# Where the second block's modulation is computed: VectorE row products in three feed-forward loops, an early half of the first norm, and turned rows

## The reference, cut to what matters

```python
cond = jax.nn.silu(c)
for i in range(DEPTH_2):                                  # 4
    mod = cond @ ada_w[i] + ada_b[i]                      # 1024 x 6144 weights, 24 MB
    sh_a, sc_a, g_a, sh_f, sc_f, g_f = jnp.split(mod, 6, axis=-1)
    h = modulate_2(rms_norm_2(x, norm_g[i, 0]), sh_a, sc_a)
    ...                                                   # y = mla, stick-breaking, retention, mla for i = 0..3
    x = x + g_a[:, None, :] * rms_norm_2(y, norm_g[i, 1])
    h = modulate_2(rms_norm_2(x, norm_g[i, 2]), sh_f, sc_f)
    y = jnp.square(jax.nn.relu(h @ ffn_w1[i])) @ ffn_w2[i]
    x = x + g_f[:, None, :] * rms_norm_2(y, norm_g[i, 3])
```

## Time and profile before

| | us |
|---|---|
| runs | 3032.50, 3034.65 and 3042.34, median 3034.65 |
| the profiled execution's own time | 3033.94 |
| its span, first to last instruction | 3031.9 |
| start of the span to the first matmul of `ab_in` | 35.1 |
| block 0: turn of its norm to the end of its attention, output projection and second norm | 1565.8 to 1720 |
| block 0: feed-forward | 1720 to 1900 |
| block 1: mixer, then feed-forward | 1904 to 2100, then to 2277 |
| block 2: mixer, then feed-forward | 2280 to 2505, then to 2720 |
| block 3: mixer, then feed-forward | 2724 to 2848, then to 3026 |

### The profile page before, as it was taken

How to read it: one execution, slowest core, us unless ns; L and a number is a source line. 1 busy time by engine, 2 the same in 40 slices (tenths; PEclk the granted TensorE clock), 3 DMA queues, 4 the chain that set the end, 5 groups by cost and what they waited for, 6 DMA issues and landing times.

```text
span 3031.9 us, 34611 instructions
## 1 busy us (share of the span) xinstructions
PE 2731.1 (90%) x13420; PEld 1704.6 (56%) x13420; DVE 1193.3 (39%) x2164; ACT 925.6 (31%) x1648; POOL 39.4 (1%) x51
## 2 busy tenths in 40 slices
PE   7999887877899889878789899998999999999999
PEld 3433422222564442222254688857888988875787
DVE  1762300001242320000033667547677465444776
ACT  2112211110212320000023544545445444444543
POOL 0010000000000000000000000000000000000000
PEclk9999999999999989999999999999999999999999
DMA  8673499999822859999986254681546425663152
GB/s 366 257 311 154 185 428 428 428 428 429 356 89 95 322 226 428 428 428 429 428 345 275 124 194 162 264 331 52 194 179 262 153 111 203 279 254 131 56 194 97
DMA packets 59496, 796.20 MB, mean 263 GB/s; under 512 B 8636, under 2 KB 9916, under 8 KB 10748
## 3 DMA queue, kind: packets, MB, share of 16 engines
q1 hardware_dynamic: 55664, 790.13, 63.4%
q10 hardware_dynamic: 3724, 4.59, 0.4%
HBM read 793.64 MB, written 1.05 MB: 262 GB/s over the span
## 4 chain that ended last, share of the span: by engine, by line
PE 74%; DMA 18%; DVE 4%; ACT 3%; issue 1%; SPq 0%; ACTq 0%; DVEq 0%; POOL 0%; POOLq 0%
PE banks L1982 12%; DMA ring<-in_t_up 7%; DMA ring<-in_t_down 7%; PE banks L1482 7%; PE banks L1999 6%; PE banks L913 6%; PE banks L1498 5%; PE banks L798 5%; PE banks L928 4%; PE banks L1357 4%; PE banks L2002 3%; PE banks L767 3%; PE banks L2006 3%; DMA arena<-in_t_gate 2%; PE banks L787 1%
## 5 line engine op out<-in xcount | busy, mean ns | idle before, releaser
L1482 PE MATMUL banks<-ring,arena 128*64 128x512 f32 x1920 | 477.2, 621 | 95.9 <-DMA ring<-in_t_up 52.2
L3043 DVE TENSOR_TENSOR ring_lo<-ring,w_hi 128x1024 fp32r<-128x1024 f32 x256 | 312.4, 1224 | 227.8 <-ACT w_hi L2414 226.7
L2414 ACT CAST w_hi<-ring 128x1024 fp32r<-128x1024 f32 x256 | 268.2, 1054 | 383.5 <-PE banks L1982 188.1
L1482 PEld LDWEIGHTS banks<-ring,arena 128*64 128x64 f32 x1920 | 161.7, 143 | 386.2 <-issue 346.6
L2601 DVE TENSOR_TENSOR arena<-arena,banks 128x512 f32<-128x512 f32 x32 | 22.0, 687 | 794.9 <-PE banks L1482 794.9
L1999 PE MATMUL banks<-u_pair,w_hi 128*128 128x512 f32 x768 | 273.3, 400 | 3.6 <-DVE ring_lo L3043 3.1
L2119 ACT COPY arena<-banks 32x512 f32 x96 | 55.3, 576 | 607.3 <-PE banks L1498 606.6
L1498 PE MATMUL banks<-ring,arena 128*64 128x512 f32 x896 | 210.3, 624 | 28.4 <-DMA ring<-in_t_down 17.1
L2002 PE MATMUL banks<-u_pair,ring_lo 128*128 128x256 f32 x768 | 215.4, 281 | 0.0
L1982 PE MATMUL banks<-w_hi,ffn_h_hi 128*128 128x512 f32 x512 | 202.3, 395 | 0.0
L1982 PE MATMUL banks<-ring_lo,ffn_h_hi 128*128 128x512 f32 x512 | 199.5, 390 | 0.0
(11 more groups left out here) (362 smaller groups left out, 4073.5 us busy)
## 6 DMA issues: line engine op xcount, KB each, us to landing
ring<-in_t_ada SPq DMA_DIRECT2D x72, 2048.0 KB, 10.0
ring<-in_t_ffn SPq DMA_DIRECT2D x64, 2048.0 KB, 8.5
ring<-in_t_gate SPq DMA_DIRECT2D x60, 2048.0 KB, 22.0
ring<-in_t_up SPq DMA_DIRECT2D x60, 2048.0 KB, 22.1
ring<-in_t_down SPq DMA_DIRECT2D x56, 2048.0 KB, 21.6
ring<-in_t_ret_in SPq DMA_DIRECT2D x12, 2048.0 KB, 8.5
arena<-in_t_down SPq DMA_DIRECT2D x8, 2048.0 KB, 31.2
ring<-in_t_in_cd SPq DMA_DIRECT2D x6, 2048.0 KB, 16.1
```

What stands on the lines that cost most here:

```text
L1482: mm = nc.tensor.matmul(PS[64 * h:64 * h + 64, f.bank, :], x_cur[:, b, k, :], wview(un[h0 + h], KC)[:, k, :], start=(k == 0), stop=(k == K ...
L2414: nc.scalar.copy(w_hi[:, n % 4], w).then_inc(S("ffn_w_hi"), 1)
L3043: TT(w_lo, w, w_hi[:, n % 4].bitcast(F32), ALU.subtract).then_inc(S("ffn_w_lo"), 1)
```

## The change

1. `ada_w_2` of layers 1 to 3 is laid out transposed (`by_outputs`, `t_ada_dots`): a tile holds, for each of 128 outputs on the partitions, four rows of 1024 weights. Bytes and number of tiles stay the same.
2. Blocks 0, 1 and 2 (`DOTS`) each load the next block's twelve tiles in their feed-forward loop, three a pass, in three slots of their own (before, two). DVE multiplies each row of 1024 with `cond_row` and sums it (`dot_dve`): twelve of these a pass, after the steps of `DOT_STEPS` and one at the end, then a copy of twelve sums to `MOD`. The tiles in `mla_pe`, `stick_pe` and the feed-forward's PE pieces go, with their ACT copies and DVE sums.
3. `cond_row` is the conditioning vector along the free axis, the same on all partitions: eight PE transposes of a broadcast column before the second norm's turn (`cond_row_pe`) and two 512-column ACT copies, once in each of blocks 0 to 2.
4. The three loops are unpaired: `PAIRED` is `(3,)`. ACT rectifies, then squares twice (rounded to `ffn_h_hi` and in float32); DVE does only the subtraction.
5. Layer 0's first four tiles are split: tiles 0 and 2 (shift and scale of chunks 0 to 3) are loaded and computed first, then the first weight tile of `ab_in`, then tiles 1 and 3, whose PE work is put after chunks 1 and 2 of the first tile of `ab_in`. DVE and ACT do the gains of chunks 4 to 7 between their own chunks 3 and 4.
6. `gp_pe` uses transposes, not matmuls.

```diff
-        plan_ada("l0a", 0, 0, 4, [0, 1, 2, 3])
+        FRONT = (("l0a", (0, 2), [0, 1, 2, 3]), ("l0d", (1, 3), [4, 5, 6, 7]))
+        plan_ada(FRONT[0][0], 0, FRONT[0][1], FRONT[0][2])
...
                 ab_units += load(turn(1), units_of(a["t_in_ab"], j))
+                if n == 0:
+                    plan_ada(FRONT[1][0], 0, FRONT[1][1], FRONT[1][2])
...
-        ADA_IN_FFN = (2,)
-        PAIRED = (0, 1, 3)
+        DOTS = (0, 1, 2)
+        PAIRED = (3,)
...
             if more:
-                fa = lambda q: (SLOT, lambda it, v=a["t_ada"][i + 3], q=q: v[it * 3 + q])
+                fa = lambda q: (SLOT, lambda it, v=a["t_ada_dots"][i], q=q: v[it * 3 + q])
                 items = [f1(0), fa(0), f1(1), fa(1), f2(0), fa(2), f2(1)]
-                slots = [s[0], s[4], s[2], s[5], s[1], s[4], s[3]]
+                slots = [s[0], s[4], s[2], s[5], s[1], s[6], s[3]]
...
+                for q, u in enumerate(au):
+                    u.used = Mark(S("dot"), 48 * i + 4 * (q + 1), 12)
...
+        cond_row = region(W + 2048, [D])
+        dots = small[:, 12:24]
...
+        def cond_row_pe(pe, i):
+
+            for half, f in enumerate(plan[f"b{i}_cb"]):
+                f.open(pe)
+                for q in range(4):
+                    mm = nc.tensor.transpose(PS[:, f.bank, q * P:(q + 1) * P],
+                                             cond[:, 4 * half + q, 2:3].to_broadcast([P, P]), ident)
+                mm.then_inc(f.full.sem, 1)
...
-                    mm = nc.tensor.matmul(PS[:, f.bank, q * P:(q + 1) * P],
-                                          GP[:, i, which, k:k + 1].to_broadcast([P, P]), ident, start=True, stop=True)
+                    mm = nc.tensor.transpose(PS[:, f.bank, q * P:(q + 1) * P],
+                                             GP[:, i, which, k:k + 1].to_broadcast([P, P]), ident)
...
+                def late_tiles(q):
+
+                    if q == 1:
+                        ada_rows_pe(late[0], late_rows[0])
+                        ada_rows_pe(late[1], late_rows[1])
+                        ada_cols_pe(late_rows[0], late_cols[0], 0)
+                    if q == 2:
+                        ada_cols_pe(late_rows[1], late_cols[1], 1)
...
-                    if s % 2 == 1 and s < 16:
-                        tile_rows(4 + s // 2)
-                    if s % 2 == 0 and s < 17:
-                        tile_cols(3 + s // 2)
...
-                    if 2 <= s < 14:
-                        ada_rows_pe(plan[p + "ada_units"][s - 2], plan[p + "ada_rows"][s - 2])
-                    if 3 <= s < 15:
-                        ada_cols_pe(plan[p + "ada_rows"][s - 3], plan[p + "ada_cols"][s - 3], (s - 3) % 2, store=st_rows)
...
+                        if i in PAIRED:
+                            act.wait_ge(S("ffn_squared"), 32 * i + k + 1 + it * 8)
+                            nc.scalar.copy(h_hi, h).then_inc(S("ffn_h_hi"), 1)
+                        else:
+                            plan[p + "up"][k].free.wait(act, it)
+                            nc.scalar.activation(h_hi, h, ACT.Square).then_inc(S("ffn_h_hi"), 1)
+                            nc.scalar.activation(h, h, ACT.Square).then_inc(S("ffn_squared"), 1)
...
+                if i in DOTS:
+                    for half, f in enumerate(plan[p + "cb"]):
+                        copy_act(act, f, cond_row[:, half * 512:half * 512 + 512], PS[:, f.bank, :])
                 ffn_hi(i, 0, 0)
...
+            DOT_STEPS = (1, 2, 3, 4, 6, 8, 10, 12, 13, 14, 15)
+
+            def dot_dve(i, n, it):
+
+                u = plan[f"b{i}_dot_units"][n // 4]
+                if n % 4 == 0:
+                    u.landed.wait(dve, it)
+                w = ring[:, u.slot, (n % 4) * D:(n % 4 + 1) * D]
+                STT(w, w, 1.0, cond_row, ALU.mult, ALU.mult, accum_out=dots[:, n:n + 1]).then_inc(S("dot"), 1)
...
+                    if i in DOTS and n in DOT_STEPS:
+                        dot_dve(i, DOT_STEPS.index(n), it)
...
+                if i in DOTS:
+                    dot_dve(i, 11, it)
+                    dve.wait_ge(S("dot"), 48 * i + 12 + it * 12)
+                    V_.tensor_copy(MOD[:, bass.ds(192 + (i + 1) * 48 + it * 12, 12)], dots).then_inc(S("dot_kept"), 1)
+                    dve.wait_ge(S("dot_kept"), 4 * i + 1 + it)
```

More of the change, by code:

```diff
@@ L553, in block_program @@
                 plan[p + "units"] = us
-                fills(p + "scores", ([0, 1, 6] * 6)[:16] if i == 0 else [0, 1, 6, 7] * 4)
+                fills(p + "scores", [0, 1, 6, 7] * 4)
                 fills(p + "turn", [2, 3] * 8)
[L556 to L563, removed]
+                fills(p + "pv", [4, 5] * 4)
                 use_split(p + "out", load(turn(2), units_of(a["t_mla_out"][j], 0, 1)), "tokens", [0, 1, 2, 3],
@@ L569, in block_program @@
                 use_split(p + "v", load(turn(2), units_of(w, 4, 5)), "tokens", [4, 5, 6, 7], st_in_slots, p + "qk")
[L570 to L575, removed]
                 fills(p + "z", [0, 1] * 8)
@@ L592, in block_program @@
             fills(p + "fnorm", [4, 5, 6, 7])
-            more = i in ADA_IN_FFN
+            more = i in DOTS
+            if more:
+                fills(p + "cb", [0, 1])
             c0 = cursor[0]
@@ L712, in pieces, with scale_dve @@
             return [(k, s) for k in range(KC) for s in range(ns)]
-        def scale_dve(dve, c, layer, which, ns, x_first=False):
-            for k, s in pieces(ns, x_first):
+        def scale_dve(dve, c, layer, which, ns, x_first=False, late=None):
+            for n, (k, s) in enumerate(pieces(ns, x_first)):
+                if late is not None and n == 4 * ns:
+                    late()
                 t = slice(s * N, (s + 1) * N)
@@ L719, in scale_dve, with shift_act @@
                                                ALU.mult, ALU.mult).then_inc(S("u_scaled"), 1)
-        def shift_act(act, c, layer, which, ns, x_first=False):
-            for k, s in pieces(ns, x_first):
+        def shift_act(act, c, layer, which, ns, x_first=False, late=None):
+            for n, (k, s) in enumerate(pieces(ns, x_first)):
+                if late is not None and n == 4 * ns:
+                    late()
                 t = slice(s * N, (s + 1) * N)
@@ L2514, in ada_dve, with front_half @@
                     f.free.wait(dve)
-            ada_dve("l0a", 0, 0)
-            gains_first(0, 0, 4, (0,))
+            def front_half(half):
+                name, tiles, _ = FRONT[half]
+                fc = plan[f"ada_{name}_cols"]
+                for f, j in zip(fc, tiles):
+                    cols_dve(f, 8 * j, 0, 0, 2)
+                for f in fc:
+                    f.free.wait(dve)
+                at = 4 * half
+                m = MOD[:, 0:32].rearrange("p (w i s) -> p w i s", w=2, s=2)[:, :, at:at + 4, :]
+                b = cols("b_ada", 0, 16).rearrange("p (w i) -> p w i", w=2)[:, :, at:at + 4]
+                ch.do(TT(m, m, b.unsqueeze(3).to_broadcast([P, 2, 4, 2]), ALU.add))
+                ch.do(STT(AM[:, 2 * at:2 * at + 8].rearrange("p (k s) -> p k s", s=2), m[:, 1], 1.0,
+                          cols("g_mix", at, 4).unsqueeze(2).to_broadcast([P, 4, 2]), ALU.add, ALU.mult))
+            front_half(0)
             def trig(x, k, rows, quarter):
@@ L3099, in _ @@
                 split_u_dve(dve, c, p + "fnorm", "ffn")
+                if i in DOTS:
+                    plan[p + "cb"][-1].free.wait(dve)
                 with dve.Fori(0, 3) as it:
```

119 lines of the change are left out of this document (33 added, 86 removed).

## The result

The changed kernel takes 3002.67 us (median of four runs, 3000.16 to 3003.30), the kernel before beside it 3033.57: a ratio of 0.9891, with a 95% interval of 0.9871 to 0.9911. This is 31 us faster, less than half of the 71 us forecast, and 7.7 us above the range's upper end. The profiled execution took 3000.16 us, its span is 2998.1 us, and its mean granted clock 0.954, against 0.972 before.

What follows compares the result with a forecast made beforehand. PE was taken as the bound outside the expert stages' DMA waits. Terms -2.5, -28.7, -7.3, -32.2, +3.3 and -4.0 sum to -71.4 from the profiled 3033.94 us; with 0.7 for the median, 2963 us, range 2947 to 2995.

Steps and rivals of the forecast that it cites:

- Block 1's attention: Block 1's attention without modulation tiles: steps of 4.50 us instead of 4.96, and no half-clock first tile; -7.3 us (-9 to 0).
- rival (b): Block 1's attention: without tiles the clock may stay at 1.2 GHz through the heads; +38 us, 3001 us; chance 0.05.
- Start: Start of the kernel: first projection begins earlier with two tiles in front, late tiles' PE work in its path; -2.5 us.
- Block 0's attention: Block 0's attention without tiles matches block 3's, and the wait for the constants shrinks; -28.7 us (-24 to -30).
- Loops: Feed-forward passes take 44.8 us with PE as bound: -32.2 us in block 2, +3.3 us in blocks 0 and 1.
- Rival (a): Feed-forward loops: row products cost double, 2.57 us each, so DVE becomes the bound; +94 us, 3057 us; chance 0.06.
- Block 3's attention: Attention of block 3, which had no tiles before: no change forecast, 0 us.
- Transposes: Transposes for `gp_pe` save 0.8 us each, five of them on PE's path in blocks 0 to 3; -4.0 us (0 to -5).
- Row of `cond`: Its eight transposes and two ACT copies before the second norm's turn are hidden in waits; 0 us (at most 1.2 a block).

Runs made afterwards that it cites:

- burst: The changed kernel with six unused f32 TensorE products behind the scores of step 3 in block 1's attention: 2996.5 us, ratio 0.9875.
- added work only: The changed kernel, VectorE's order as it is, with three unused TensorE products behind the scores of steps 1 and 2 in block 1's attention: 2994.1 us.
- the start alone: The kernel before with only the first four modulation tiles split and the late tiles between the first projection's chunks: 3030.6 us, ratio 0.9975.
- the reordered kernel with added work: The changed kernel with VectorE's softplus sum moved ahead and three unused TensorE products behind the scores of steps 1 and 2, block 1's attention: 2945.3 us.
- products twice: The changed kernel with each VectorE row product made twice, so block 1 to 3 modulation is wrong: 3074.1 us, ratio 1.0131.
- one product in every step: The changed kernel with one unused TensorE product behind the scores in each of steps 2 to 15 of block 1's attention: 2968.8 us, ratio 0.9789.
- transposes undone: The changed kernel with the gain rows of blocks 0 to 3 made by matmuls with the identity again: 3002.8 us.
- no products: The changed kernel with its VectorE row products replaced by one-element instructions, so block 1 to 3 modulation is wrong: 2994.8 us.
- order: The changed kernel with VectorE's softplus sum of head s-1 put ahead of reading head s's scores in block 1's attention: 2949.8 us, ratio 0.9723.
- block 1's part undone: The changed kernel with block 1's modulation back as TensorE tiles in its attention and its feed-forward loop paired again: 2972.1 us, ratio 0.9795.
- the order in the kernel before: The kernel before with VectorE's softplus sum moved ahead in block 1's attention, modulation tiles left on TensorE: 3033.0 us, ratio 0.9995.

## Why the prediction was wrong

**Block 1's attention is the step that failed.** "Here PE's tile work ran while PE would have waited for DVE's chain, so most of it was free": true, and it was also what kept the clock at 1.00. I took the 4.50 us of the one step without tile rows for all of them. That step lay right behind 55 us of work without a gap, and as the kernels with a burst and with added work show, one or two steps behind such work do take 4.50, and then the clock falls. In the kernel before the attention ended before that: its few remaining steps kept 1.00. The attention without its tiles gave +25.2 us for -7.3, and steps of 6.83 us for 4.50. My rival (b) had this mechanism. That its time, 3001 us, lies so near the 3002.7 measured is in part luck: its +38 over the forecast was 32.5 here, and the other terms missed by 5.1 in sum, misses of up to 5 us either way. It went wrong in its chance, 0.05, for a reason that can be named. "The last heads run with the same share at 1.00, so that share holds the clock once up" was read from one 5-us window, and a busy share in a window that follows full work shows nothing about what holds. With 13 steps at risk it should have had some 0.3 to 0.4, and the range should have reached over 3001.

The other terms, in order:

- **Start**, -2.5 for -6.3 to -7.7. The first product started at 25.88, earlier than the 27.4 that I had worked out, and the clock in the first chunks, 0.66 before at 35 to 40 us, stayed at 1.00. The price of the late tiles was right: 3.57 + 0.59 + 0.44 = 4.6 us for the 4.7 forecast. In the start alone the same part gave 3.2 us, near the forecast, so some 3 of the 6.3 are the first DMA's and the clock's chance.
- **Block 0's attention**, -28.7 for -25.8. The attention loop gave 26.5 for 26.3. The wait for the constants is gone, and the query projection starts 9.06 us earlier, 1.4 of that its own gain. But at 1585 to 1590 us the clock is 0.50, and this projection takes 18.40 us for 16.35.
- **Loops**, right to a few tenths of a us a pass: 44.82 for 44.8, +4.4 for +3.3 in blocks 0 and 1, and -33.0 for -32.2 in block 2. The product takes 1.22 us for the 1.4 that I took, and DVE is busy 36.18 us a pass for my 38.6. Rival (a), double the price, is refuted; what the Trainium skill says in "Vector Engine (DVE) Microarchitecture Reference", Points that are easy to get wrong, is not so here: the product with two float32 sources takes 1.219 us for 1024 elements, the subtraction beside it 1.225. The point from which DVE decides, 1.92 us each, is by the starts (44.8 - 21.4)/12 = 1.95, with 21.4 = 18.2 + 2.7 + 0.5 for all but the products. With 2.40 for a pair of products it was over it and the kernel slower than before, as the rival said.
- **Block 3's attention**, 0 for +4.2. In the profile of after the clock is 0.50 at 2745 to 2750 us, behind a wait of 1.04 us:

```profile
2745.00:2750.00 5.00, 4.94 (x14) 2.46 (x13) 3.33 (x15) 2.38 (x10) 0.00 (x0) 0.50 0.00 0
```

  From the value products to the output projection this takes 41.9 us; over all profiles it is either 41.9 to 42.2 (after, the start alone, the reordered kernel with added work, added work only, products twice) or 38.3 to 38.5 (before and the other seven). Both groups hold kernels with and without the change, and the code of this stretch is the same in all but for the gain rows at its end. So the heads' 3.5 us can't be laid to a part of the change. The clock is lost in other places too: the query projection ahead of the heads takes 18.14 us for 16.55 in four profiles (burst, one product in every step, transposes undone, no products), the first quarter behind them 7.3 for 5.7 in three (burst, order, block 1's part undone). Only before and the order in the kernel before lose it in none of the three places. What decides is open.
- **Transposes**, -4.0 for nothing measurable. Each turned pair is 0.9 to 1.0 us shorter, as forecast, but in the kernel after two first quarters, of blocks 0 and 1, at half clock take back 1.6 each.
- **Row of `cond`**, 0: ACT still waits 1.97 us for the turn of block 0's second norm (2.94 before).

A granted clock below 1.00 is in most of these misses, the product's price and a part of the start's apart: I had treated it as fixed where before had it, while the change altered what stands between the waits.

## What to carry to other kernels

Work that stands in another engine's wait isn't free to take away when it keeps TensorE at work: before removing it, look at the steps without it and ask whether the clock was ever tested there for longer than a few steps. Then look at what the wait is made of; here it was two instructions in a queue ahead of the one that TensorE needed, and moving that one brought 53 us once the tiles were gone, and nothing while they were there to fill the wait. Where such a wait can't be removed, products whose results nobody uses can be worth more than they cost.

## What the chip showed that was not expected

- In the loop with 1.71 us of waiting in each step of 6.83 the clock stayed at 0.50 for some 99 us. In the same loop without the waits (VectorE's order) it was 0.95 at 1970 to 1975 us, and with one product in each wait 0.77 at 1960 to 1965 us, and from there 1.00 to the end.
- From 1.00, the same loop at 4.50 us a step lost the clock within two steps, twice (burst: 1980 to 1985 us, added work only: 1965 to 1970 us). At the end of the attention in the kernel before, from 2050 to 2060 us, it kept it with 3.29 of 5 us busy.
- DVE's starts lie 1.14 us apart for instructions of 1.22. Reading out the sum of a product (0.08 us) adds nothing that the profile shows when the next instruction doesn't need it (1.15 from start to start), and a product that waits for the one before it starts after 1.25.
- Fourteen unused products lowered the whole by 34 us, 1.1%; the attention in which they stand is 30.4 us shorter.
